# Attention scores as two fp32r passes over stacked high and low parts, in an encoder layer on one NeuronCore

## The reference

```python
proj = u @ w_in                       # -> qa ka va | qb kb vb, 8 heads of 64 each
# group A: dilated windows (128,1), (512,4), (2048,16), distance penalty, merged by log-sum-exp
# group B: windows of 8 x 16 on a 16 x 64 grid of tokens, with a learned bias
s = einsum(q, k) * 64 ** -0.5         # scores
p = softmax(s + bias)
y = concat(p_a @ v_a, p_b @ v_b) @ w_out
```

## Time and profile before

| what | us |
|---|---|
| median of 3 runs | 2078.88 (2078.32 to 2079.28) |
| the profiled execution, its own time | 2078.98 |
| span of its trace | 2077.2 |
| PE busy | 1959.9 (94%) |
| DVE busy, ACT busy | 1195.8 (58%), 801.3 (39%) |
| first score of group A, last score of group A | 797.53, 1040.33 |
| first score of group B, last score of group B | 1092.97, 1292.68 |

### The profile page before, as it was taken

The page is one execution under the profiler, slowest core; times in us unless marked ns, Lnnn a source line. Parts: engine busy times, 40 slices in busy tenths (PEclk is TensorE's granted clock), DMA queues, the critical chain, the costliest instruction groups (busy, mean ns, idle before and its releaser), DMA issues. The chain is left out here.

```text
span 2077.2 us, 27306 instructions
## 1 busy us (share of the span) xinstructions
PE 1959.9 (94%) x9962; PEld 1532.6 (74%) x9962; DVE 1195.8 (58%) x2056; ACT 801.3 (39%) x1397; POOL 606.4 (29%) x433
## 2 busy tenths in 40 slices
PE   6899999999999969999889997889999999999996
PEld 4677777777888747777567775778788888887884
DVE  5855555555686963344424445587744444457778
ACT  4533333333445363343413434336433333334541
POOL 0353444333960010000041331001543443449300
PEclk9999999999999989999999999999999999999998
DMA  9255454555874323111042220612233323367732
GB/s 318 64 192 163 163 180 160 179 166 171 317 246 144 101 62 100 30 42 41 11 106 50 41 61 31 233 71 92 95 114 102 108 95 102 117 227 264 251 99 102
DMA packets 184885, 270.56 MB, mean 130 GB/s; under 512 B 12592, under 2 KB 111152, under 8 KB 184624
## 3 DMA queue, kind: packets, MB, share of 16 engines
q1 hardware_dynamic: 153888, 235.18, 33.8%
q10 hardware_dynamic: 29840, 29.50, 4.5%
q0 software_dynamic: 1024, 4.13, 1.2%
HBM read 210.84 MB, written 57.93 MB: 129 GB/s over the span
## 5 line engine op out<-in xcount | busy, mean ns | idle before, releaser
L1581 PE MATMUL f_ps<-f_uh,f_ops 128*128 128x512 f32 x2496 | 783.0, 392 | 13.1 <-DVE f_ops L1272 4.2
L1581 PEld LDWEIGHTS f_ps<-f_uh,f_ops 128*128 128x128 f32 x2496 | 469.6, 188 | 127.5 <-issue 24.1
L1581 PE MATMUL f_ps<-f_ul,f_ops 128*128 128x512 f32 x1248 | 487.6, 391 | 0.0
L966 POOL TENSOR_TENSOR f_sums<-f_raw 128x512 f32<-128x512 f32 x80 | 113.0, 1413 | 547.6 <-DVE f_ul L1401 238.0
L1581 PEld LDWEIGHTS f_ps<-f_ul,f_ops 128*128 128x128 f32 x1248 | 235.0, 188 | 47.6
L1431 DVE TENSOR_TENSOR f_dl<-f_blocks,f_dh 128x1024 fp32r<-128x1024 f32 (+1 forms) x146 | 202.4, 1401 | 81.5 <-ACT f_dh L1162 81.1
L1162 ACT CAST f_dh<-f_blocks 128x1024 fp32r<-128x1024 f32 (+1 forms) x146 | 144.3, 990 | 228.2 <-PE f_ps L1715 225.6
L1715 PE MATMUL f_ps<-f_dh 128*128 128x512 f32 x496 | 196.1, 395 | 9.3 <-DVE f_ev L1465 4.9
L1272 DVE TENSOR_TENSOR f_ops<-f_sums,f_ops 128x512 fp32r<-128x512 f32 x160 | 119.6, 748 | 139.8 <-ACT f_ops L1027 139.7
L1715 PE MATMUL f_ps<-f_dh,f_dl 128*128 128x512 f32 x496 | 194.7, 393 | 0.0
L1715 PE MATMUL f_ps<-f_dl,f_dh 128*128 128x512 f32 x496 | 194.7, 393 | 0.0
(11 more groups left out here) (249 smaller groups left out, 2987.3 us busy)
## 6 DMA issues: line engine op xcount, KB each, us to landing
f_hidden<-acc SPq DMA_DIRECT2D x154, 256.0 KB, 3.8
f_blocks<-f_hidden SPq DMA_DIRECT2D x154, 256.0 KB, 3.5
f_blocks<-in_ffn_w_down SPq DMA_DIRECT2D x132, 256.0 KB, 6.0
f_raw<-in_ffn_w_gate SPq DMA_DIRECT2D x20, 1024.0 KB, 6.1
f_raw<-in_ffn_w_up SPq DMA_DIRECT2D x20, 1024.0 KB, 5.3
f_aw<-in_w_ada ACTq DMA_DIRECT2D x28, 512.0 KB, 3.6
acc<-in_w_ada ACTq DMA_DIRECT2D x28, 512.0 KB, 4.7
in_raw<-in_w_in SPq DMA_DIRECT2D x24, 512.0 KB, 3.9
```

The lines of the kernel that those rows point to most:

```text
L966: nc.gpsimd.tensor_tensor(sums[:, x], of, with_, how).then_inc(s_done, 1)
L1581: done = nc.tensor.matmul(ps[:, bank, :], l[:, k, :], r[:, k, :], start=fresh and k == 0 and m == 0, stop=closed and k == HK - 1 and m == ...
```

## The change

1. Keys: `keys` gets a copy for each head. For head i its own 64 rows hold the scaled key rounded to fp32r (written by ACT), the other 64 rows the remainder (written by DVE, which subtracts ACT's result from the PSUM output and so waits for ACT).
2. Queries: `q` holds the rounded query of a head in both halves of the rows (ACT, four copies for each output), `q_lo` the remainder (DVE, after ACT). In group A both also write the unrounded query into `q_full` for the class matmuls, which stay as they are.
3. A score over the band (A) or the window (B) is two fp32r matmuls into one PSUM result: q over 128 rows (high times high and high times low), and `q_lo` over the head's 64 rows.
4. Order: keys, values, queries instead of keys, queries, values; `q` has one buffer instead of two. Both engines now take both halves of keys and queries; DVE takes values one step later.
5. The softmax is divided in place in a ring of three `ex` tiles instead of into `pn`; the exponential waits for the transposes of unit u - 3. Fewer memsets on GpSimd; `y` of group A lies in scratch.

```diff
-        return [(j, half) for j in (1, 0, 2) for half in range(HALVES)]
+        return [(j, half) for j in (1, 2, 0) for half in range(HALVES)]
...
-        q = a.sb(tag + "_q", [P, 2, 2, S])
-        keys = a.sb(tag + "_k", [P, 2, S])
+        q = a.sb(tag + "_q", [P, 2, S], F32R)
+        q_lo = a.sb(tag + "_q_lo", [P, S], F32R)
+        keys = a.sb(tag + "_k", [P, 2, 2, S], F32R)
...
+            q_full = a.sb("a_q_full", [P, 2, S])
...
# ScalarE: exponential
+                if u >= 3:
+                    act.wait_ge(p_tr, u - 2)
+                nc.scalar.activation(ex[:, u % 3, :], t_s[:, b, :], ACT.Exp, bias=sm[:, b, 0:1], scale=-1.0,
...
# ScalarE: take
+                elif j == 1:
+                    for head in range(2):
+                        ins = nc.scalar.activation(keys[rows_of(head), head, p % 2, key_columns(half)],
+                                                   out[rows_of(head)], ACT.Copy, scale=-HD ** -0.5)
+                    if dil and half == 1:
+                        ins = nc.scalar.activation(class_keys(p, half), class_out(out), ACT.Copy, scale=-HD ** -0.5)
+                    ins.then_inc(pj_s, 1)
+                else:
+                    queries_free(act, p, half)
+                    for head in range(2):
+                        for rows in (rows_of(head), other_rows(head)):
+                            ins = nc.scalar.copy(query_columns(q[rows, head, :], half),
+                                                 query_out(out[rows_of(head)]))
+                    if dil:
+                        ins = nc.scalar.copy(query_columns(q_full[rows_of(1), 1, :], half), query_out(out[rows_of(1)]))
+                    ins.then_inc(pj_s, 1)
...
# VectorE: division
-                if u >= 4:
-                    dve.wait_ge(p_tr, u - 3)
-                nc.vector.tensor_scalar(pn[:, b, :], ex[:, b, :], sm[:, b, 2:3], None,
+                part = ex[:, (u - 2) % 3, :]
+                nc.vector.tensor_scalar(part, part, sm[:, b, 2:3], None, ALU.mult).then_inc(divided, 1)
...
# VectorE: take
+                dve.wait_ge(pj_s, taken(n, False))
+                for head in range(2):
+                    rows = rows_of(head)
+                    if j == 1:
+                        cols = key_columns(half)
+                        ins = nc.vector.scalar_tensor_tensor(keys[other_rows(head), head, p % 2, cols], out[rows],
+                                                             -HD ** -0.5, keys[rows, head, p % 2, cols].bitcast(F32),
+                                                             ALU.mult, ALU.subtract)
+                    else:
+                        ins = nc.vector.tensor_tensor(query_columns(q_lo[rows, :], half), query_out(out[rows]),
+                                                      query_columns(q[rows, head, :], half).bitcast(F32),
+                                                      ALU.subtract)
+                if dil and j == 1 and half == 0:
+                    ins = nc.vector.tensor_scalar(class_keys(p, half), class_out(out), -HD ** -0.5, None, ALU.mult)
+                if dil and j == 0:
+                    ins = nc.vector.tensor_copy(query_columns(q_full[rows_of(0), 0, :], half), query_out(out[rows_of(0)]))
+                ins.then_inc(pj_v, 1)
...
                 if s < U + 2:
                     step(s)
+                for g, i in ended_in(s - 2):
+                    if outputs(g)[i][0] == 2:
+                        take(g, i)
                 for g, i in ended_in(s - 1):
-                    take(g, i, dve)
+                    if outputs(g)[i][0] != 2:
+                        take(g, i)
...
# TensorE: score
                 if m == 0:
+                    wait_taken(output_at(p, 0, 0))
+                if m == (NU // 2 if dil else 2):
                     wait_taken(output_at(p, 0, 1))
...
+                passes = ((slice(0, P), q[:, i, :]), (rows_of(i), q_lo[rows_of(i), :]))
+                for n, (rows, own) in enumerate(passes):
+                    if dil:
+                        w0 = band_start(t)
+                        nc.tensor.matmul(sc[:, b, 0:BAND], own[:, P * t:P * t + P], keys[rows, i, p % 2, w0:w0 + BAND],
+                                         start=n == 0, stop=n == 1, skip_group_check=True)
```

More of the change, by code:

```diff
@@ L1833, in taken @@
             j, half = outputs(m // NPJ)[m % NPJ]
-            count += j == 0 or (half == 0) == by_vector
+            count += j != 2 or (half == 0) == by_vector
         return count
     def split_at(g, j):
-        return 3 * (g - 1) + ((2, 1, 0) if g == 1 else (1, 0, 2)).index(j) + 1
+        return 3 * (g - 1) + ((2, 1, 0) if g == 1 else (1, 2, 0)).index(j) + 1
     def values_due(s):
@@ L1898, in bank @@
             return o[:, 0, :] if bank_of(n) == 2 else pj[:, bank_of(n), :]
[L1900 to L1928, removed]
-            else:
[L1930 to L1938, removed]
@@ new lines, in rows_of, with other_rows, query_columns, query_out @@
+        def rows_of(head):
+            return slice(HD * head, HD * head + HD)
+        def other_rows(head):
+            return rows_of(1 - head)
+        def query_columns(of, half):
+            if dil:
+                return of[:, NB * half:NB * half + NB].rearrange("p (t r m) -> p t r m", r=CL, m=CQ)
+            return of.rearrange("p (c b r w) -> p c b r w", c=CBS, b=RBS, r=QR)[:, :, half]
+        def query_out(out):
+            if dil:
+                return out.rearrange("p (t m r) -> p t r m", r=CL, m=CQ)
+            return out.rearrange("p (r c w) -> p c r w", r=QR, c=CBS)
@@ new lines, in key_columns, with queries_free, take_values @@
+        def key_columns(half):
+            return slice(NB * half, NB * half + NB)
+        def queries_free(eng, p, half):
+            if p >= 1:
+                last = (HT, TT)[half] if dil else (TT - 1, TT)[half]
+                eng.wait_ge(qk, NU * (p - 1) + 2 * last)
+        def take_values(p, half, eng, copy, done):
+            out = bank(output_at(p, 2, half))
+            if p >= 1:
+                eng.wait_ge(v_tr, NVG * p)
+            if dil:
+                ins = copy(v[:, NB * half:NB * half + NB], out)
+            else:
+                for cb in range(CBS):
+                    ins = copy(vc[:, cb, QR * half:QR * half + QR, :],
+                               out.rearrange("p (r c) -> p r c", c=COLS)[:, :, KC0[cb]:KC0[cb] + KC])
+            ins.then_inc(done, 1)
@@ L1940, in _, with class_keys, class_out @@
+        def class_keys(p, half):
+            m0 = CK // HALVES * half
+            return kc[:, p % 2, :, m0:m0 + CK // HALVES]
+        def class_out(out):
+            return out.rearrange("p (m r) -> p r m", r=CL)
         @block.sync
@@ L1983, in _ @@
         def _(pool):
-            for i in range(2):
-                for par in range(2):
-                    nc.gpsimd.memset(q[HD * (1 - i):HD * (2 - i), par, i, :], 0.0).then_inc(zeroed, 1)
             if dil:
+                for i in range(2):
+                    nc.gpsimd.memset(q_full[other_rows(i), i, :], 0.0).then_inc(zeroed, 1)
                 return
-            pool.wait_ge(zeroed, 4)
             for p in range(HP):
@@ L2037, in turned_out, with take @@
                                tr[:, turn_at["t", u] % 2, 0:W].rearrange("p (c q) -> p c q", c=NC)).then_inc(p_out, 1)
-            take(0, 2, act)
+            def take(p, i):
+                j, half = outputs(p)[i]
+                if j == 2 and half == 0:
+                    return
+                act.wait_ge(pj_mm, NPJ * p + i + 1)
+                out = bank(NPJ * p + i)
+                if j == 2:
+                    take_values(p, half, act, nc.scalar.copy, pj_s)
+                elif j == 1:
[11 more added lines that the diff above has]
+                                                 query_out(out[rows_of(head)]))
+                    if dil:
+                        ins = nc.scalar.copy(query_columns(q_full[rows_of(1), 1, :], half), query_out(out[rows_of(1)]))
+                    ins.then_inc(pj_s, 1)
+            take(0, 1)
+            take(0, 2)
             split(1, 2)
-            take(0, 3, act)
+            take(0, 3)
             split(1, 1)
-            take(0, 4, act)
-            take(0, 5, act)
+            take(0, 4)
+            take(0, 5)
             for s in range(U + LAG):
@@ L2150, in output, with take @@
                 ins.then_inc(y_out, 1)
-            take(0, 0, dve)
-            take(0, 1, dve)
+            def take(p, i):
+                j, half = outputs(p)[i]
+                if j == 2 and half == 1:
+                    return
+                n = NPJ * p + i
+                out = bank(n)
+                if j == 2:
+                    dve.wait_ge(pj_mm, n + 1)
+                    take_values(p, half, dve, nc.vector.tensor_copy, pj_v)
+                    return
+                dve.wait_ge(pj_s, taken(n, False))
[15 more added lines that the diff above has]
+                ins.then_inc(pj_v, 1)
```

(23 more changed lines are left out.)

23 lines of the change are left out of this document (10 added, 13 removed).

## The result

The changed kernel takes 2153.71 us in the median (2149.36 to 2154.64, 4 runs) against 2079.08 for the one before: a ratio of 1.0355, 95% interval 1.0337 to 1.0373. It is slower, as forecast, but by 74.6 us instead of the 34.7 that the prediction adds up. The profiled execution took 2152.8 us, its span is 2151.0, 73.8 more than before.

A forecast was written before the change was run, and what follows sets the result against it. PE's list was taken to bound each step where scores run beside projections. The terms 2 + 13.3 + 5.4 + 7.9 + 2.7 + 3.4 = 34.7 us, added to 2078.98, gave 2113 us, 80% range 2080 to 2123.

The forecast's parts named there:

- the sign: Whole kernel: slower than before, chance 0.83; faster 0.08, within 0.2% 0.09.
- the passes in a step: Score passes on PE, tile changes costing time: 0.01 us gained a step in A, 0.05 lost in B, together +2 us.
- The rival of free changes: Score passes: changes of row tiles cost nothing, passes give back 28.5 us, stalls stay; 2088 us, chance 25%.
- item 2: Keys, half 1, m = 6, pairs 1 and 2: value copy behind DVE's take stalls PE 3.65 and 3.0 us, +13.3 us.
- item 1: Keys, half 0, m = 3: DVE's take behind ACT ends in time in A and B, hidden, no cost.
- Item 6: Start of each phase: first value copy waits 2.4 us (A), 1.9 (B), first score saves 0.82 each; +2.7 us.
- the list of costs of nothing: Other edits, such as division in place, one `q` buffer, later values, fewer memsets: no time added.
- items 3 and 4: Queries, halves 0 and 1, m = 14 and 0: late takes stall pairs 1 and 2, +5.4 us.
- item 5: Start of pair 3: the same query waits, with no projections on PE to fill them, +7.9 us.
- item 7: Clock: lower level after the four stalls of item 2, +3.4 us, bounds nothing and 7.

The follow-up runs named there:

- the one with the takes alone: Changed kernel with its new takes of projection outputs, but each band or window score one plain fp32 matmul over 128 rows: 2142.82 us, ratio 1.0304.
- best: Changed kernel, DVE takes one step later, other banks in pair 0 of A, first value copies earlier, B's second pass over 128 rows: 2091.09 us, ratio 1.0046.

## Why the prediction was right or wrong

- **Right: the sign, and the passes in a step.** 3.66 and 3.09 us a step, unchanged in A and 0.05 more in B (0.01 less and 0.05 more forecast); with free tile changes 3.46 and 2.75 were forecast and 3.47 and 2.75 measured. The rival of free changes falls, since the changes cost what the rows of column tiles gave. Over the whole program the passes were mis-sized: 2 us forecast, 5.8 for the passes alone, 3.3 of it in the last pair of B, where the sum had no clock.
- **Right: item 2.** Stalls of 3.65 and 3.0 forecast, 3.83 and 2.9 measured: 13.4 us for the four, 13.3 forecast.
- **Wrong: item 1, "Hidden" for keys, half 0, m = 3.** I counted ACT as free at T + 3.67 in every step, but at m = 3 and 11 it waits for `multiply`. Put at nothing; 5.9 us for the four.
- **Item 6: its waits right, one left out.** The waits for the first value copies grow by 2.8 us in A and 2.2 in B (2.4 and 1.9 forecast), and the first score saves its 0.82. But item 6 looked at which take the first score waits for and not at which bank the first projection of the next pair wants; this wait stands neither there nor in the list of costs of nothing, and takes 6.0 us (the run with other banks).
- **Mis-sized: items 3 and 4**, 5.4 forecast, 10.1 measured. Five copies on ACT took 2.95 us and not 2.5, two subtractions and a copy on DVE 2.1 and not 1.8: the sum had each start some 0.09 us before the last one's end, and they don't (last section).
- **Mis-sized: item 5**, 7.9 forecast, 17.3 measured for both last pairs. In A turn(48) comes 14.3 us after step 48 was due, where 12.3 were forecast: 6.7 more than before and not 4.7, and of these 2.0 the longer copies of two takes are 1.5. The other 1.6 of A's 8.3 us come later, at the lower clock level: the 56 matmuls of `multiply` take 5.75 us instead of 3.71. In B 6.1 of the 9.0 us are at m = 15 to 4 and 2.9 after that, where the kernel with the passes alone is 3.4 longer and the one with the takes alone 1.7; how much is wait and how much clock was not told apart.
- **Mis-sized: item 7.** 3.4 us for the clock, with 7 as the bound. The filled stalls alone give 6.4 us back, and the 87 us more at the lower level leave room for up to 44 in all. I counted only the four stalls of item 2; the granted clock is also 0.57 around the first step (806 to 814) and at the start of both last pairs (1038 to 1050, 1325 to 1337). This and the missed waits put the time out of the range, whose upper end held the clock's cost to 3.4 more.

That DVE's wait for ACT is the cause of most of the loss is shown by the run without it (53 us); taking DVE's part a step later gives 24, since other work then stands in line. That the clock has a part of its own is shown by the filled stall. How the remaining loss in the changed kernel divides between waits and clock, outside m = 6 and 7, stays open.

## What to carry to other kernels

When an operation is split so that a second engine needs the first one's result, don't put its part in the same step: it blocks everything behind it in that engine's list for as long as the first engine is late. Give it a step of distance, and put copies for which PE waits ahead of takes and splits. Of each engine list, look at every step that has a wait of its own (here `multiply`), and at each buffer's next writer. Where PE was busy without a gap, count every new gap of some 3 us for itself and, with another 1 to 2 us, for the clock. A pass over fewer rows can be slower than one over all rows with zeros: in B the step is 3.09 us with 64 rows and 2.76 with 128 (`best`).

## What the runs showed of the hardware that was not expected

- The copies on 64 rows that follow one another here don't overlap: four on ACT take 2.35 us (0.59 apart, their full length) and two on DVE 1.39, while before the change two copies of 128 rows from the same PSUM bank started 0.47 apart on ACT (a_kc at 889.32, a_k at 889.79) and 0.60 on DVE. Each of these copies also reads or writes other rows than the one before it, and writes fp32r; which of the three keeps them apart wasn't tested.
- A stall of 2.9 to 3.8 us cost another 1 to 2 us through the clock in the step after it; 2.6 to 3.3 us of other matmuls put into it cost nothing and gave that back.
- Going from a tile of 128 rows to one of 64 rows and back costs 0.34 us a time in B, as much as two passes of 384 columns, and 0.20 in A.
- The fp32r passes cost time by the clock as well: in the run with the passes alone, the granted clock in B's last pair is 0.66 between 1268 and 1289, where it is 1.00 in the kernel before, and the step of m = 7 takes 3.70 us instead of 2.95.
